# Sparse-attention input projection as three rounded products from its fifth weight slot on, with the split made by ScalarE and GpSimd

## What is computed

```python
for l in range(DEPTH):                                  # DEPTH = 2
    h = x @ w_in[l] + b_in[l]                           # x: 256 x 1024
    lru_x, lru_gate, q, kc_raw, vc_raw, ks_, vs_, kw_, vw_, gts = jnp.split(h, offsets, axis=-1)
    y_lru = _rg_lru(lru_x, lru_gate, ...)
    y_nsa = _nsa(q, kc, vc, ks_, vs_, kw_, vw_, gts)
    mix = jnp.concatenate([_rms_norm(y_lru, ...), _rms_norm(y_nsa, ...)], axis=-1) @ w_out[l]
    x = _layer_norm(ALPHA * x + mix, ...)
    x = _layer_norm(ALPHA * x + _peer(x, ...), ...)
```

## Time and profile before

| | |
|---|---|
| median of 3 runs | 3184.26 us (3180.24 to 3185.0) |
| the profiled execution, its device time | 3183.18 us |
| its span | 3181.4 us |
| TensorE busy | 3099.9 us (97%) |
| VectorE, ScalarE, GpSimd busy | 2060.5 (65%), 1442.3 (45%), 162.8 us (5%) |
| granted TensorE clock, mean | 0.991 |
| HBM read | 611.66 MB, 193 GB/s over the span |
| input projection of `nsa` (L2149), both layers | 146.6 us of TensorE |
| `nsa`, layer 0: first projection product to start of the next stage | 1084.98 to 1256.14 us |
| `nsa`, layer 1: the same | 2131.04 to 2300.33 us |

### The profile page before, as it was taken

One profiled execution on the slowest core, in us unless ns is written; L12 is line 12 of the kernel. 1 busy time (PEld: TensorE's weight loads), 2 busy tenths in 40 slices (PEclk: granted clock), 3 DMA queues, 4 the chain that ended last, 5 costly groups with the idle time before them and its releaser, 6 DMA issues.

```text
span 3181.4 us, 46656 instructions
## 1 busy us (share of the span) xinstructions
PE 3099.9 (97%) x15882; PEld 2577.3 (81%) x15882; DVE 2060.5 (65%) x4022; ACT 1442.3 (45%) x2307; POOL 162.8 (5%) x297
## 2 busy tenths in 40 slices
PE   8999999999999998999999999999999999999998
PEld 6698876768886787888888888878788978888887
DVE  5567752636773252989677667665288966766666
ACT  2436642436663143156345454444415634445454
POOL 3100000200000000410000000000032000000000
PEclk9999999999999999999999999999999999999999
DMA  8648896835889522423556555643243255556553
GB/s 324 245 177 310 294 345 263 299 103 200 303 316 352 222 87 84 139 87 108 189 191 192 187 193 188 192 168 112 78 139 98 99 181 191 191 189 193 186 194 122
DMA packets 167140, 614.71 MB, mean 193 GB/s; under 512 B 18753, under 2 KB 18785, under 8 KB 166097
## 3 DMA queue, kind: packets, MB, share of 16 engines
q1 hardware_dynamic: 151632, 551.62, 50.9%
q0 software_dynamic: 15360, 61.16, 5.1%
HBM read 611.66 MB, written 1.05 MB: 193 GB/s over the span
## 4 chain that ended last, share of the span: by engine, by line
PE 86%; DVE 8%; ACT 3%; DMA 1%; DVEq 1%; issue 1%; POOL 0%; ACTq 0%; POOLq 0%
PE PS L1623 13%; PE PS L1624 13%; PE PS L1625 13%; PE PS L2269 11%; PE PS L2271 6%; PE PS L1669 4%; PE PS L2252 4%; PE PS L2231 3%; PE PS L2149 3%; PE PS L1683 2%; PE PS L1710 2%; PE PS L1951 2%; PE PS L2137 2%; DVE arena L1489 1%; DVE arena L1490 1%; PE PS L2000 1%
## 5 line engine op out<-in xcount | busy, mean ns | idle before, releaser
L1009 DVE TENSOR_TENSOR w_lo<-arena,w_hi 128x1024 fp32r<-128x1024 f32 x448 | 529.9, 1219 | 0.0
L605 ACT ACTIVATE w_hi<-arena 128x1024 fp32r<-128x1024 f32 x448 | 451.6, 1049 | 105.5 <-DMA arena<-in_v_t 62.5
L1623 PE MATMUL PS<-w_hi,pw_hi 128*128 128x512 f32 x1024 | 403.3, 394 | 7.2 <-DVE w_lo L1009 6.7
L1624 PE MATMUL PS<-w_lo,pw_hi 128*128 128x512 f32 x1024 | 402.1, 393 | 0.0
L1625 PE MATMUL PS<-w_hi,pw_lo 128*128 128x512 f32 x1024 | 399.6, 390 | 0.0
L2269 PE MATMUL PS<-x_lh,w_hi 128*128 128x512 f32 x1536 | 379.4, 389 | 0.0
L2269 PEld LDWEIGHTS PS<-x_lh,w_hi 128*128 128x128 f32 x1536 | 288.2, 188 | 59.7
L949 ACT ACTIVATE arena<-PS 128x256 f32<-128x256 f32 x192 | 73.9, 385 | 446.9 <-PE PS L2271 446.9
L1230 DVE TENSOR_TENSOR gu_lo<-raw,gu_hi 128x1024 fp32r<-128x1024 f32 x192 | 222.5, 1220 | 19.1 <-ACT gu_hi L693 19.1
L2231 PE MATMUL PS<-x,arena 128*128 128x256 f32 x896 | 229.5, 384 | 3.8 <-ACT arena L888 3.8
L1623 PEld LDWEIGHTS PS<-w_hi,pw_hi 128*128 128x128 f32 x1024 | 193.6, 189 | 44.3 <-issue 7.8
(11 more groups left out here) (415 smaller groups left out, 5242.7 us busy)
## 6 DMA issues: line engine op xcount, KB each, us to landing
arena<-in_u_t SPq DMA_DIRECT2D x256, 512.0 KB, 4.5
arena<-in_v_t SPq DMA_DIRECT2D x256, 512.0 KB, 3.6
raw<-in_w_gu SPq DMA_DIRECT2D x192, 512.0 KB, 5.4
arena<-in_w SPq DMA_DIRECT2D x152, 512.0 KB, 3.6
arena<-in_w_ada POOLq DMA_DIRECT2D x96, 512.0 KB, 6.9
raw<-in_w_down SPq DMA_DIRECT2D x96, 512.0 KB, 5.6
arena<-in_w_gu SPq DMA_DIRECT2D x64, 512.0 KB, 7.3
arena<-in_w_down SPq DMA_DIRECT2D x32, 512.0 KB, 4.8
```

What stands on the lines that cost most here:

```text
L605: A(w_hi[:, m % RING], ring[:, m % RING], ACT.Copy).then_inc(S["hi_done"], 1)
L1009: V.tensor_tensor(w_lo[:, m % RING], ring[:, m % RING], w_hi[:, m % RING].bitcast(F32), ALU.subtract)\
L1623: mm(dst, w[0], m[0], start=start, stop=False)
L1624: mm(dst, w[0], m[1], start=False, stop=False)
```

## The change

In both `nsa` stages the input projection's slots 4 to 19 (16 of 20) are made as three rounded products in place of float32 ones; slots 0 to 3 stay as they are.

- **ScalarE** rounds `x` once (`xn_hi`, 128 x 2048) at the stage's start, and then each of the 16 weight slots (`weights_hi(i)`, one copy of 128 x 1024). These copies stand at fixed places between its other work; `evac(6)` is moved ahead of `exps(2)`. From slot 8 on a copy waits until TensorE has finished slot i - 4, whose rounded weights lay in the same buffer.
- **VectorE** makes the remainder of `x` (`xn_lo`, 128 x 2048) ahead of its work on `lam`.
- **GpSimd** makes the remainder of each weight slot (`nsa_weights_lo`, one subtraction of 128 x 1024, both inputs in SBUF), after ScalarE's copy; from slot 10 on it also waits for TensorE to finish slot i - 4.
- **TensorE** waits for `lo_done` in place of the load, and issues 24 matmuls of 128 x 256 for a slot in place of 16.
- **SyncE** loads a slot again when the remainder is made (`lo_done`) in place of `slot_done`.
- A small buffer, `ast`, moves to another place of the arena. Nothing else in the program changes.

```diff
 OUT_BANK = (4, 5, 0, 1)
+W2_PLAIN = 4
+W2_SPLIT = W2_IN - W2_PLAIN
 EARLY, EARLY_1, LATE = 32, 16, 4
...
         N["sv"] = [s0[:, 0:SLOT], s0[:, SLOT:], *(arena[:, RING_AT + n * SLOT:RING_AT + (n + 1) * SLOT] for n in (4, 5, 9, 10))]
-        N["ast"] = arena[:, RING_AT + 8 * SLOT:RING_AT + 8 * SLOT + 18 * NH].rearrange("p (u a b) -> p u a b", u=6, b=NH)
+        N["ast"] = arena[:, RING_AT + 13 * SLOT:RING_AT + 13 * SLOT + 18 * NH].rearrange("p (u a b) -> p u a b", u=6, b=NH)
         N["rs"] = N["blk"].rearrange("p a m c -> p (a m c)")[:, 0:2 * T]
+        xn_hi = rounded("xn_hi", "h", 0, [KT, T])
+        xn_lo = rounded("xn_lo", "arena", RING_AT + 11 * SLOT, [KT, T])
+
+        def wn_places():
+            pt, wtm, r, i = (N_AT[name][0] for name in ("pt", "wtm", "r", "i"))
+            wa = N_AT["x2"][0] + X2["wa"][0]
+            hi = [RING_AT + (6, 7, 8, 10)[n % 4] * SLOT for n in range(W2_SPLIT - 1)] + [i]
+            lo = [pt + n * SLOT for n in range(6)] + [wtm, wtm + SLOT, wa, RING_AT + 9 * SLOT, wtm, wtm + SLOT, wa, r, wtm, wtm + SLOT]
+            return hi, lo
+        wn_hi, wn_lo = ([rounded(f"wn_{w}{n}", "arena", at, [SLOT]) for n, at in enumerate(ats)]
+                        for w, ats in zip(("hi", "lo"), wn_places()))
...
             SPLIT[k, l] = at
-            at += {"peer": PEER_SLOTS}.get(k, 0)
+            at += {"peer": PEER_SLOTS, "nsa": W2_SPLIT}.get(k, 0)
         LN = {s: i for i, s in enumerate([s for s in plan if s[0] in ("nsa", "peer")])}
...
+        def nsa_split(n):
+
+            for kind, l in plan:
+                m = n - BASE[kind, l] - W2_PLAIN
+                if kind == "nsa" and 0 <= m < W2_SPLIT:
+                    return SPLIT[kind, l] + m + 1
+            return None
+
         @block.sync
...
                     sp.wait_ge(S["lo_done"], SPLIT[kind] + n - RING - BASE_SPLIT[kind] + 1)
+                elif nsa_split(n - RING):
+                    sp.wait_ge(S["lo_done"], nsa_split(n - RING))
                 elif n >= RING:
...
                     last.then_inc(S["pk_ab"], 1)
+
+            def nsa_weights_lo(l):
+                n0 = BASE["nsa", l]
+                for i in range(W2_PLAIN, W2_IN):
+                    m = i - W2_PLAIN
+                    pool.wait_ge(S["hi_done"], SPLIT["nsa", l] + m + 1)
+                    if m >= 6:
+                        pool.wait_ge(S["slot_done"], n0 + i - 3)
+                    if i == 17:
+                        pool.wait_ge(S["th_ok"], l + 1)
+                    nc.gpsimd.tensor_tensor(wn_lo[m][:], ring[:, (n0 + i) % RING], wn_hi[m][:].bitcast(F32), ALU.subtract)\
+                        .then_inc(S["lo_done"], 1)
...
                 A(lam[:, 1], lam[:, 0], ACT.Exp, scale=-1.0).then_inc(S["lam_e"], 1)
+                A(xn_hi[:], x[:], ACT.Copy).then_inc(S["xs_hi"], 1)
+
+                def weights_hi(*tiles):
+                    for i in tiles:
+                        n = n0 + i
+                        wait_slot(act, n)
+                        if i >= W2_PLAIN + 4:
+                            act.wait_ge(S["slot_done"], n - 3)
+                        A(wn_hi[i - W2_PLAIN][:], ring[:, n % RING], ACT.Copy).then_inc(S["hi_done"], 1)
...
                 evac(0)
+                weights_hi(4, 5)
                 evac(1)
+                weights_hi(6, 7)
                 evac(2)
+                weights_hi(8, 9)
                 act.wait_ge(S["ri_mm"], l + 1)
...
                 A(N["u"], N["r"], ACT.Tanh).then_inc(S["th_ok"], 1)
+                weights_hi(10)
                 evac(3)
+                weights_hi(11, 12)
                 evac(4)
+                weights_hi(13)
                 act.wait_ge(S["u_in"], l + 1)
                 A(N["u"], N["a1"], ACT.Sqrt).then_inc(S["sqrt_ok"], 1)
+                weights_hi(14)
                 exps(0)
                 evac(5)
+                weights_hi(15)
                 exps(1)
+                weights_hi(16)
                 turned(0)
+                evac(6)
+                weights_hi(17)
                 exps(2)
-                evac(6)
+                weights_hi(18)
                 turned(1)
                 evac(7)
+                weights_hi(19)
                 turned(2)
...
                 dve.drain()
+                dve.wait_ge(S["xs_hi"], l + 1)
+                V.tensor_tensor(xn_lo[:], x[:], xn_hi[:].bitcast(F32), ALU.subtract).then_inc(S["xs_ok"], 1)
                 V.reciprocal(lam[:, 3], lam[:, 2])
...
                         pe.wait_ge(S["pair_evac"], p0 + j - 1)
-                    wait_slot(pe, n0 + i)
-                    for k in range(KT):
-                        if i == 0:
-                            wait_x(pe, ("nsa", l), k)
-                        last = mm(PS[:, j % 2, T * q:T * q + T], ring[:, (n0 + i) % RING, P * k:P * k + P], x[:, k],
-                                  start=k == 0, stop=k == KT - 1)
+                    dst, m = PS[:, j % 2, T * q:T * q + T], i - W2_PLAIN
+                    if m >= 0:
+                        pe.wait_ge(S["lo_done"], SPLIT["nsa", l] + m + 1)
+                        if m == 0:
+                            pe.wait_ge(S["xs_ok"], LN["nsa", l] + 1)
+                        for k in range(KT):
+                            last = mm3(dst, (wn_hi[m][:, P * k:P * k + P], wn_lo[m][:, P * k:P * k + P]), (xn_hi[:, k], xn_lo[:, k]),
+                                       k == 0, k == KT - 1)
+                    else:
+                        wait_slot(pe, n0 + i)
+                        for k in range(KT):
+                            if i == 0:
+                                wait_x(pe, ("nsa", l), k)
+                            last = mm(dst, ring[:, (n0 + i) % RING, P * k:P * k + P], x[:, k], start=k == 0, stop=k == KT - 1)
                     last.then_inc(S["slot_done"], 1)
```

More of the change, by code:

```diff
@@ L180 @@
 ps_mm ps_ev pk_ci pk_ab pk_exp pk_top pk_t pk_tev pt_a pt_b pt_mm g_ev y2t z2_ok pk_ok p_ok ag_ok gelu_ok up_lo up_sum pw_ok tab_load hi_done
-lo_done xs_ok y2_ev out_st""".split()
+lo_done xs_hi xs_ok y2_ev out_st""".split()
 def program(nc, a, out, plan=None, dumps=None):
@@ L289, in program @@
         ], RING_AT + 11264)
-        N = area([
+        n_items = [
             ("p", (W2_IN, T)), ("wtm", (KT, TMW)), ("x2", (X2_N,)), ("vtm", (TT, 4 * HD)), ("gt", (TT, 3 * NH)),
@@ L294, in program @@
             ("gvr", (P,)), ("kc", (2 * NC,)), ("vcz", (4, HD)), ("cs", (TT, NH, 32)), ("ct", (4, P)), ("st", (3, TT * NH)),
-            ("s0", (NH, T)), ("pt", (6 * NH, P)),
+            ("s0", (NH, T)), ("pad", (6,)), ("pt", (6 * NH, P)),
             ("tab", (TAB_N - 384,)),
-        ])
+        ]
+        N, N_AT = area(n_items), _layout([(name, int(np.prod(dims))) for name, dims in n_items])[0]
         N["mix"] = arena[:, 5120:7168].rearrange("p (a b) -> p a b", b=T)
@@ L566, in _ @@
                         pool.dma_start(N["tab"], a["tab"][:, 384:]).then_inc(S["tab_load"], 16)
+                        nsa_weights_lo(l)
                     else:
@@ L2284, in peer @@
                 n = n0 + EARLY
-                pe.wait_ge(S["xs_ok"], l + 1)
+                pe.wait_ge(S["xs_ok"], LN["peer", l] + 1)
                 for j in range(PEER_STEP):
```

## The result

| | before | after |
|---|---|---|
| median of 4 runs each | 3183.44 us (3180.24 to 3185.0) | 3232.06 us (3228.38 to 3233.03) |
| ratio, 95% interval | | 1.0151 [1.0135, 1.0166] |
| span of the profiled execution | 3181.4 us | 3231.2 us |
| granted TensorE clock, mean | 0.991 | 0.981 |
| `nsa`, first slot to the next stage's first product, layer 0 | 164.02 us | 188.51 us |

The change makes the kernel 48.6 us slower (1.5%), and the two stages account for 48.8 of the profiled executions' difference (the next stage's first product is the sum of squares, L1654 before and L1713 after; this measure ends some 7 us before that of the table ahead of the prediction).

A forecast was written before the change was run, and what follows sets the result against it. TensorE (97% busy) was taken as the bound, with the attention chain or DMA already as late in places. Per layer 2.2 walk + 1.0 contention + 0.4 clock, twice: +7 us, 3191 us; own range 3183 to 3197, wider 3181 to 3206.

The forecast's parts named there:

- the walk: Event-by-event forecast of layer 0's stage against before: 13.4 us of new waits against 11.2 saved, +2.2 at its end.
- The gain, one slot: TensorE's projection slots: 2.86 us rounded for 3.56 plain, saving 0.7 us each, 22 us over two layers.
- GpSimd's 2.4 us: Assumed length of GpSimd's remainder subtraction for each weight slot, bounds 1.2 to 2.9 us, under TensorE's 2.86 us.
- Item 1: Slots 4 and 5: slot 4 waits about 4 us, slot 5 ends +2.9 us, gates() doesn't wait for the convolution.
- Items 3 to 5: turn(0), scores(2), scores(3): new TensorE waits of 2.8, 3.0 and 2.3 us, bringing the delay to +1.7, +3.7, +4.7.
- item 2: Slots 6 to 9: remainders made during gates() and values(), saving 2.8 us; slot 10 starts +0.5 us.
- item 6: Slots 15 to 19 and the stage's end: no new wait through slot 17, +2.6, then +2.2 us at the end.
- Contention: VectorE operations with two SBUF inputs held up by GpSimd's new subtractions: 1 us a layer, bounds 0 to 7.
- Clock: TensorE's half-speed clock invited behind the new waits: 0.4 us a layer, bounds 0 to 3.5.
- Contention rules: Rival: GpSimd's operations at 2.9 us block VectorE at each meeting, +6 us a layer, 3198 to 3206; chance 0.10.
- GpSimd's stall: Rival: GpSimd's first subtraction stalls at slot 4 in layer 0, TensorE some 7 us later, 3198; chance 0.18.
- The gain survives: Rival: ScalarE's copies fall in idle time and chain waits stay as before, -16 us, 3168; chance 0.10.

The follow-up runs named there:

- run 2: Changed kernel with GpSimd's subtraction cut to 8 columns and the third product taking rounded weights instead of the remainder: 3196.76 us, ratio 1.0051.
- run 10: Changed kernel with only slots 6 to 9 rounded, GpSimd making their remainders after waiting for the convolution: 3178.11 us, ratio 0.9983.
- Run 1: Changed kernel with evac(1) ahead of the rounding copies of slots 4 and 5 in ScalarE's list: 3220.43 us, ratio 1.0118.
- run 7: Changed kernel with slots 4 and 5 left plain (14 rounded slots) and GpSimd waiting for the convolution before its first subtraction: 3206.34 us, ratio 1.0068.
- run 8: Kernel of run 2 with ScalarE's slot copies moved behind exps or turned, and exps(2) ahead of evac(6) again: 3184.16 us, ratio 0.9997.
- run 6: Kernel of run 2 with two GpSimd memsets of the whole remainder tile ahead of the 8-column subtraction: 3211.87 us, ratio 1.0095.
- runs 3 and 4: Kernel before the change plus GpSimd work nobody waits for, from evac(1) on: four subtractions of 128 x 896 (3182.02 us), or twelve memsets of 128 x 1024 (3183.38 us).
- run 9: Changed kernel, nothing taken out, with small filler matmuls inside TensorE's waits: 3218.35 us, ratio 1.0099.
- run 5: Kernel of run 2 with 8 or 9 small filler matmuls ahead of each of six TensorE waits: 3186.88 us, ratio 1.0019.
- run 4: Kernel before the change plus twelve GpSimd memsets of 128 x 1024 from evac(1) on, which read nothing and nobody waits for: 3183.38 us.

## Why the prediction was wrong

The direction and most of the walk were right; the size was not, +48.6 us for +7. The step that failed is the contention of GpSimd with VectorE: the walk had the convolution done just ahead of gates(), and the sum had 1 us a layer for contention, where the runs show about 16. By its steps:

- *The gain, one slot* (0.7 us): a rounded slot takes 3.06 us from its start to the start of what follows, a plain one 3.65 (slot 10 in runs 2 and 10); four in a row take 11.62 for 13.98. That is 0.6 us, 19 us in all for 22: the 0.119 us between matmuls is right, the change-over at a slot's ends was left out. With run 10 the gain itself is shown: it survives where the new steps lie under other work.
- *GpSimd's 2.4 us*: 2.34 to 2.40, but for a few held up themselves, at most 2.87. *The wait at slot 4* "of about 4 us": 3.93.
- *Item 1, "the convolution behind it, 4.5 us ..., so gates() doesn't wait for it"*: **the step that failed first**. The walk itself set slot 5's copy ahead of evac(1) and so moved the convolution into the time in which GpSimd has the remainders of slots 5 to 9 to make. It took 13.0 us, gates() waited 8.35, and item 1 came to +14 in place of +2.9 in layer 0. Run 1 shows the order's part, run 7 that of the place as a whole (23 to 26 us in both layers).
- *Items 3 to 5*: waits of 2.8, 3.0 and 2.3 us forecast, 3.87, 2.21 and 2.21 found. 1.4 us of turn(0)'s is contention (2.51 in run 2). That ScalarE's order stands in this chain is shown by run 8: moving the copies, and evac(6) with them, takes 12.6 us away in both layers. Fewer waits also leave fewer slow stretches: windows of 2 us with a granted clock under 1 are some 40 us of layer 0's stage in run 2 and 20 in run 8 (22 and 16 in layer 1). In its own arithmetic the walk has two slips: item 2's terms, +2.9 - 2.8, give +0.1 and not +0.5, and item 6 goes from +2.6 to +2.2 without a term. They cancel.
- *Contention*, "I take 1 us a layer", bounds 0 to 7: **the term that was mis-sized**. Run 2 puts it at 31 us by the stages, 14.7 and 16.6 a layer, with the slow clock that it brings; run 6 excludes latency as its cause, runs 3 and 4 show the mechanism without the change. The bound counted one meeting at each of three places. A place isn't one operation: the convolution is eight short ones, and each may wait for a whole subtraction, so the bound there is GpSimd's queue (five times 2.4 us), not 2.4. And "most of the places find GpSimd idle or near its end" was never walked through; the copies of slots 5 to 9 were in the walk, and GpSimd's five subtractions follow from them.
- *Clock*, "I take 0.4", bounds 0 to 3.5 a layer: mis-sized too. 11 to 14 us in after (run 9), 10 to 13 in run 2's kernel (run 5), 5 to 7 a layer. A stretch at 0.50 follows nearly every wait over 2 us. Up to turn(0) it cost run 2 next to nothing, as "where TensorE is early anyway" says; behind turn(0) it slowed the transposes and scores that the next wait hangs on, and the work behind scores(3).
- *The rivals*: "Contention rules" named the right mechanism but gave it 3198 to 3206, by the same count of places. GpSimd's stall didn't strike in after at slot 4 (the 9.39 us of the earlier trace rows stayed in peer); run 6 has it at slot 4, where it costs TensorE more than this rival feared (12.81 us of waiting for run 2's 1.94). "The gain survives" failed as said, at turn(0) and before.

The parts overlap (a slow stretch follows a wait that contention made), so runs 2, 7, 8 and 9 don't add up to 49, and how much of the slow clock belongs to contention wasn't separated.

## What to carry to other kernels

Before giving a second engine work beside VectorE, lay its operations on VectorE's timeline one by one: a short operation can cost the whole length of the other engine's instruction, so a chain of many short ones is the worst neighbour, and the bound is the length of GpSimd's queue, not one instruction for each place. Give a cheaper form of the work only to those slots whose preparation fits under work that is there anyway (four of twenty here), and keep the preparation out of chains that already end last. Price each new wait with the slow clock behind it: here that was about a quarter of the loss.

## What the runs showed of the hardware

- VectorE beside GpSimd's subtraction: held are operations with two SBUF inputs (L1408, L1428) and `tensor_scalar` in SBUF (L1403, L1430, even L1447 with eight elements: 2.03 for 0.17 us). Not held are the reciprocal (6.55 us) and, beside the subtraction of 1163.29 to 1165.68, L1442 with one input in PSUM (1.22) and the reduction L1445 (1.22). Beside a memset only `tensor_scalar` is held (2.15 for 0.73 and 5.05 for 1.14, run 4), two-input operations are not (L1355 2.78, L1363 1.21).
- GpSimd is held too: two subtractions took 5.81 us for 4.67 beside one VectorE product of 1.22 us (run 10).
- GpSimd's stall without a releaser moves with the program. In before, after and every run but 4 and 6 it is 9.39 us at the first L531 of layer 0's peer (L554 of after). In runs 4 and 6, the two with memsets in `nsa`, that place has 0.24 us and the stall is among the memsets: 9.29 between the fourth and the fifth in run 4 (2.17 in layer 1), 9.29 and 6.82 between the first two in run 6. What sets its place wasn't tried.
- Filler matmuls in waits were worth 10 us in run 5 (waits of 2 to 4 us) and 14 in run 9 by the medians, though each adds work to TensorE.
